# Queries of the differential attention turned by VectorE and DMA, with the scores moved almost a block later

## What is computed

```
k, v = split(rms_norm(x) @ w_kv);  k = rms_norm(k per 128 columns)
q = rms_norm((rms_norm(x) @ w_q) per 128 columns) * 128 ** -0.5
s = q @ k.T + alibi bias, causal;   p = softmax(s)
a = p[component 0] - lambda * p[component 1]
o = a @ v;   o = rms_norm(o per head);   x = x + o @ w_out
```

## Time and profile before

| quantity | value |
|---|---|
| median of 3 runs | 2207.62 us (2207.1 to 2207.95) |
| the profiled execution | 2208.22 us |
| its span, first to last instruction | 2206.4 us |
| TensorE matmul busy | 2194.8 us, 99% |
| VectorE busy | 1235.3 us, 56% |
| ScalarE busy | 1057.9 us, 48% |
| granted TensorE clock, mean | 1.00 |

### The profile page before, as it was taken

How to read it: one execution, slowest core, us unless ns; L and a number is a source line. 1 busy time by engine, 2 the same in 40 slices (tenths; PEclk the granted TensorE clock), 3 DMA queues, 4 the chain that set the end, 5 groups by cost and what they waited for, 6 DMA issues and landing times.

```text
span 2206.4 us, 27194 instructions
## 1 busy us (share of the span) xinstructions
PE 2194.8 (99%) x9766; PEld 1814.4 (82%) x9766; DVE 1235.3 (56%) x1448; ACT 1057.9 (48%) x1428; POOL 38.5 (2%) x66
## 2 busy tenths in 40 slices
PE   8999999999999999999999999999999999999999
PEld 7888778888888888888888888888888888888887
DVE  5666556655555555555566675665555555555443
ACT  5666455444444444444456665554444444444332
POOL 1000000000000000000000000000000000000000
PEclk9999999999999999999999999999999999999999
DMA  7766667776767666666666555677676767666654
GB/s 244 214 193 173 175 211 216 203 216 193 215 200 210 205 203 205 199 206 200 204 198 212 180 157 180 209 221 209 198 214 197 216 192 216 198 214 193 194 193 162
DMA packets 254194, 443.34 MB, mean 201 GB/s; under 512 B 25600, under 2 KB 51168, under 8 KB 254112
## 3 DMA queue, kind: packets, MB, share of 16 engines
q1 hardware_dynamic: 253472, 440.95, 66.4%
q0 software_dynamic: 368, 0.79, 0.2%
q10 hardware_dynamic: 272, 0.52, 0.1%
HBM read 414.37 MB, written 2.10 MB: 189 GB/s over the span
## 4 chain that ended last, share of the span: by engine, by line
PE 97%; DVE 1%; DMA 1%; SPq 0%; ACT 0%; issue 0%; DVEq 0%; ACTq 0%
PE acc L603 32%; PE acc L605 32%; PE acc L604 32%; PE tps L614 0%; PE side L807 0%; DMA x<-in_x 0%; DVE w_lo L1246 0%; DVE g_oT L1280 0%; DMA tok<-g_r 0%; SPq L474 0%; DMA raw<-in_gla_w_in 0%; PE side L652 0%; PE side L705 0%; PE side L687 0%; PE side L805 0%
## 5 line engine op out<-in xcount | busy, mean ns | idle before, releaser
L1246 DVE TENSOR_TENSOR w_lo<-raw,w_hi 128x1024 fp32r<-128x1024 f32 x784 | 954.9, 1223 | 842.0 <-ACT w_hi L879 837.8
L879 ACT ACTIVATE w_hi<-raw 128x1024 fp32r<-128x1024 f32 x784 | 827.6, 1060 | 1009.1 <-PE acc L605 999.8
L603 PE MATMUL acc<-w_hi,xT 128*128 128x512 f32 x2048 | 801.9, 392 | 0.1
L605 PE MATMUL acc<-w_hi,xT 128*128 128x512 f32 x2048 | 797.9, 390 | 0.0
L604 PE MATMUL acc<-w_lo,xT 128*128 128x512 f32 x2048 | 797.8, 390 | 0.0
L603 PEld LDWEIGHTS acc<-w_hi,xT 128*128 128x128 f32 x2048 | 385.0, 188 | 80.6 <-issue 1.2
L605 PEld LDWEIGHTS acc<-w_hi,xT 128*128 128x128 f32 x2048 | 384.9, 188 | 80.5
L604 PEld LDWEIGHTS acc<-w_lo,xT 128*128 128x128 f32 x2048 | 385.1, 188 | 80.0 <-issue 0.7
L605 PE MATMUL acc<-w_hi,hT 128*128 128x512 f32 x704 | 273.9, 389 | 0.0
L604 PE MATMUL acc<-w_lo,hT 128*128 128x512 f32 x704 | 273.9, 389 | 0.0
L603 PE MATMUL acc<-w_hi,hT 128*128 128x512 f32 x704 | 273.9, 389 | 0.0
(11 more groups left out here) (179 smaller groups left out, 1048.8 us busy)
## 6 DMA issues: line engine op xcount, KB each, us to landing
raw<-in_ffn_w_in SPq DMA_DIRECT2D x352, 512.0 KB, 4.1
raw<-in_ffn_w_out SPq DMA_DIRECT2D x176, 512.0 KB, 4.9
raw<-in_gla_w_in SPq DMA_DIRECT2D x96, 512.0 KB, 4.2
raw<-in_w_kv SPq DMA_DIRECT2D x64, 512.0 KB, 4.4
raw<-in_gla_w_out SPq DMA_DIRECT2D x32, 512.0 KB, 5.0
raw<-in_diff_w_q SPq DMA_DIRECT2D x32, 512.0 KB, 4.8
raw<-in_diff_w_out SPq DMA_DIRECT2D x32, 512.0 KB, 5.0
tok<-scratch SPq DMA_DIRECT2D x496, 32.0 KB, 3.2
```

The source lines that it names most:

```text
L603: nc.tensor.matmul(acc[p][tb][:, :], hi, w_hi[:, slot, j, :], start=(kt + j == 0), stop=False)
L605: last = nc.tensor.matmul(acc[p][tb][:, :], lo, w_hi[:, slot, j, :], start=False, stop=(kt + j == n_kt - 1))
L879: nc.scalar.activation(w_hi[:, slot, :, :], raw[:, slot, :, :], ACT.Copy).then_inc(hi_done, 1)
L1246: nc.vector.tensor_tensor(w_lo[:, slot, :, :], raw[:, slot, :, :], w_hi[:, slot, :, :].bitcast(F32), ALU.subtract).then_inc(lo_done, 1)
```

## The change

The queries now take the keys' path: VectorE transposes squares of `tok` into a new buffer `q_squares`, 16 DMAs for each block move them into `d_v`, and ScalarE copies them to `d_q`, at (6,3), (7,3), (8,3) and (9,3). TensorE's 32 transposes of queries are gone. The scores, softmaxes and exponentials of even heads move from (5..8, 6) to (6..8, 5) and (9,6), those of odd heads from (6..8, 1) and (9,0) to (7..10, 1) on TensorE (VectorE and ScalarE: (b,2), before (9,0) for the last). The turning of the weights moves from (6..8, 5) and (9,3) to (7..10, 5). The first value product, `diff_output(0)`, moves from (9,2) to (9,3), and the second from (10,1) to (10,3), their squares to (9,4) and (10,4); `diff_o_out` moves from k = 4 to k = 5. Since the last scores now stand between the value products, `scores(6)` waits for `o_tok` of `diff_output(0)`, and `diff_output(1)` for `s_max` of softmax(7). The squares of the first value product go into `q_squares`, because `scratch` still serves the softmaxes.

```diff
+    for n in range(4):
+        units["diff_q", n] = UNIT0["diff_in"] + UB * (n + 5) + 1
     for n in range(3):
-        units["diff_o", n] = UNIT0["diff_in"] + UB * (9 + n) + 4
+        units["diff_o", n] = UNIT0["diff_in"] + UB * (9 + n) + 5
...
+            if name == "diff_q":
+                return qs_in, k_at[n % 2]
+            if name == "diff_o" and n == 0:
+                return qs_in, squares_at
...
                 if h % 2 == 0:
-                    for half in range(2):
-                        pe.wait_ge(t_free[half], PAIR["diff_q", h // 2] + 1)
+                    pe.wait_ge(k_turned, 4 + h // 2 + 1)
+                if h == 6:
+                    pe.wait_ge(o_tok, H_G + 1)
...
-                if n == 0:
-                    pe.wait_ge(s_max, H_D)
+                if n < 2:
+                    pe.wait_ge(s_max, (6, H_D)[n])
                 else:
                     pe.wait_ge(o_tok, H_G + n)
...
-                    if 6 <= b <= 9 and k == (1 if b < 9 else 0):
-                        scores(2 * (b - 6) + 1)
-                    if b >= 9 and k == (2 if b == 9 else 1):
+                    if 7 <= b <= 10 and k == 1:
+                        scores(2 * (b - 7) + 1)
+                    if b >= 9 and k == (3 if b < 11 else 1):
                         diff_output(b - 9)
...
-                    if 6 <= b <= 9 and k == (5 if b < 9 else 3):
-                        probs_turn(b - 6)
-                    if 5 <= b <= 8 and k == (4 if b < 6 else 3):
-                        pe.wait_ge(evacuated[(b - 1) % 2], evac_count("diff_in", b - 1))
-                        transpose_block(PAIR["diff_q", b - 5], tok)
-                    if 5 <= b <= 8 and k == 6:
-                        scores(2 * (b - 5))
+                    if 7 <= b <= 10 and k == 5:
+                        probs_turn(b - 7)
+                    if 6 <= b <= 9 and k == (5 if b < 9 else 6):
+                        scores(2 * (b - 6))
...
                     if k == 3 and 2 <= b <= 5:
-                        k_out(b - 2)
+                        heads_out("diff_k", b - 2, d_k, "k")
+                    if k == 3 and 6 <= b <= 9:
+                        heads_out("diff_q", b - 6, d_q, "q_scaled")
...
-                if n < 4:
-                    dve.wait_ge(evacuated[n % 2], evac_count("diff_in", n))
-                    if n:
-                        all_moved(dve, "diff_k", n - 1)
-                    turn("diff_k", n, lambda tb: tok[:, tb, :])
+                dve.wait_ge(evacuated[n % 2], evac_count("diff_in", n))
+                name, j = ("diff_k", n) if n < 4 else ("diff_q", n - 4)
+                if j:
+                    all_moved(dve, name, j - 1)
+                turn(name, j, lambda tb: tok[:, tb, :])
...
-                    if 10 <= b and k == 4:
+                    if 10 <= b and k == 5:
                         turned_low("diff_o", b - 10, d_oT, diff_o_gain)
-                    if 9 <= b and k == 4:
+                    if 9 <= b and k == 5:
                         diff_o_out(b - 9)
```

More of the change, by code:

```diff
@@ L81, in transpose_jobs @@
     order += [("ffn0_x", 3, True)]
[L82 to L85, removed]
+    order += [("probs", n, False) for n in range(4)]
     pair, split = {}, {}
@@ L139 @@
 TURN = {job: n for n, job in enumerate(TURN_UNIT)}
-TURN_SPLIT = {job: n for n, job in enumerate(job for job in TURN_UNIT if job[0] not in ("gla_qk", "diff_k"))}
+TURN_SPLIT = {job: n for n, job in enumerate(job for job in TURN_UNIT if job[0] not in ("gla_qk", "diff_k", "diff_q"))}
 XQ_SPOT = [(2, 6), (3, 6), (0, 5), (0, 7)]
@@ L275, in trunk @@
             d_oT = sb("d_oT", [P, 2, KT, S], F32R, s1)
+            q_squares = sb("q_squares", [P, TB * CB], F32, s1)
         acc = [[ctx.enter_context(nc.psum_tensor(f"acc{p}{tb}", [P, CB], F32)) for tb in range(TB)] for p in range(2)]
@@ L378, in trunk @@
         k_at = [landing(d_v[:, n, :, :]) for n in range(2)]
+        qs_in = leaving(q_squares[:, :])
         q_in = leaving(d_q[:, 0:TB * CB // S, :].rearrange("q a n -> q (a n)"))
@@ L470, in move_turned @@
                             sp.wait_ge(k_turned, n - 1)
+                        if name == "diff_q":
+                            sp.wait_ge(k_turned, n + 3)
                     if 0 <= first < MOVES:
@@ L1143, in diff_o_gain, with heads_out @@
                 return GAIN["diff_head_scaled"] + kt % 2
-            def k_out(n):
-                all_moved(act, "diff_k", n)
+            def heads_out(name, n, dst, gain):
+                all_moved(act, name, n)
                 for tb in range(TB):
-                    dst = d_k[:, 4 * n:4 * n + 4, tb * P:(tb + 1) * P].rearrange("q k (s t) -> q k s t", t=SQ)
-                    last = nc.scalar.activation(dst, turned(tb, k_at[n % 2]), ACT.Copy, scale=gains[:, GAIN["k"]:GAIN["k"] + 1])
+                    at = dst[:, 4 * n:4 * n + 4, tb * P:(tb + 1) * P].rearrange("q k (s t) -> q k s t", t=SQ)
+                    last = nc.scalar.activation(at, turned(tb, k_at[n % 2]), ACT.Copy, scale=gains[:, GAIN[gain]:GAIN[gain] + 1])
                 last.then_inc(k_turned, 1)
@@ L1195, in _ @@
                         diff_v_out(b - 9)
-                    if 6 <= b <= 9 and k == (2 if b < 9 else 0):
-                        row_exps(2 * (b - 6) + 1)
-                    if 9 <= b and k == (3 if b == 9 else 2):
+                    if 7 <= b <= 10 and k == 2:
+                        row_exps(2 * (b - 7) + 1)
+                    if 9 <= b and k == (4 if b < 11 else 2):
                         diff_o_squares(b - 9)
[L1200 to L1207, removed]
-                    if 10 <= b and k == 4:
+                    if 7 <= b <= 10 and k == 6:
+                        probs_out(b - 7)
+                    if 10 <= b and k == 5:
                         turned_high("diff_o", b - 10, d_oT, diff_o_gain)
@@ L1212, in _ @@
                             xq_high(n)
-                    if 5 <= b <= 8 and k == 6:
-                        row_exps(2 * (b - 5))
+                    if 6 <= b <= 9 and k == (5 if b < 9 else 6):
+                        row_exps(2 * (b - 6))
                     split_ahead(UNIT0["diff_in"] + b * UB + k)
@@ L1370, in scores_out @@
                 nc.vector.tensor_copy(g_at[:, h, 2, :], side[0][:, 3 * P:4 * P]).then_inc(at_free, 1)
-            def tok_is_free(pair):
-                for half in range(2):
-                    dve.wait_ge(t_done[half], pair + 1)
             def gla_o_out(h):
@@ L1547, in qk_norm @@
                 dve.wait_ge(g_rstd_ready, n + 1)
-                if n >= 5:
-                    tok_is_free(PAIR["diff_q", n - 5])
                 for tb in range(TB):
@@ L1607, in diff_o_out @@
                 if n == 0:
-                    tok_is_free(PAIR["diff_q", 3])
+                    all_moved(dve, "diff_q", 3)
                 dve.wait_ge(o_rstd_ready, H_G + n + 1)
@@ L1630, in _ @@
                         qk_norm(b - 1)
-                    if 6 <= b <= 9 and k == (2 if b < 9 else 0):
-                        softmax(2 * (b - 6) + 1)
-                    if 10 <= b and k == 4:
+                    if 7 <= b <= 10 and k == 2:
+                        softmax(2 * (b - 7) + 1)
+                    if 10 <= b and k == 5:
                         turned_low("diff_o", b - 10, d_oT, diff_o_gain)
-                    if 9 <= b and k == 4:
+                    if 9 <= b and k == 5:
                         diff_o_out(b - 9)
@@ L1639, in _ @@
                             xq_low(n)
-                    if 5 <= b <= 8 and k == 6:
-                        softmax(2 * (b - 5))
+                    if 6 <= b <= 9 and k == (5 if b < 9 else 6):
+                        softmax(2 * (b - 6))
                     split_ahead(UNIT0["diff_in"] + b * UB + k)
```

## The result

The changed kernel takes 2212.2 us, median of 12 runs (2209.78 to 2213.74), against 2207.61 us of before (12 runs): ratio 1.0019, 95% interval 1.0011 to 1.0026. It is a small loss, 4.6 us (2.4 to 5.7 by the interval), clear of no change; the bound of 0.2% that I had set for "slower" lies inside the interval. The forecast was 2211.4.

A forecast was written before the change was run, and what follows sets the result against it. TensorE, busy 99% of the span and holding 97% of the chain, was taken as the bound. Waits of 7.25 us against 3.5 us removed gave +3.75 us, so 2207.62 + 3.8 = 2211.4 us, range 2208.8 to 2213.6.

The forecast's parts named there:

- What is removed: Four turnings of queries, 0.87 us each, leave TensorE: 3.5 us off; nothing else leaves it.
- rival 3: Each TensorE transpose is worth its 272 ns duration, so 32 are 8.7 us: 2206.2 us; chance 0.02.
- The waits of the value products: diff_output(0) at (9,3) and diff_output(1) at (10,3) wait for s_max of the softmax: 2.2 us each, 4.4 us.
- The waits for the weights of the softmax: TensorE's turning of weights waits at (7,5) for 0.95 us and at (8,5) for 1.2 us.
- scores(6): At (9,6) TensorE waits for tok of diff_output(0): 0.7 us.
- Sum: Over the five TensorE waits: 7.25 us of waits against 3.5 us removed, +3.75 us.
- rival 4: TensorE's clock falls in the two 2.2 us waits, 1.8 us for each warming: 2215 us; chance 0.05.
- rival 1: Weight loads come late for ScalarE in block 9, 1 to 2 us in one or two places: 2213.2 us; chance 0.14.

The follow-up runs named there:

- order only: Changed kernel's late order, but queries still turned by TensorE with 32 transposes, no squares or small DMAs for them: 2213.76 us, 1.0029 of before.
- the doubled squares: Changed kernel with VectorE's transposes of squares done twice for the queries of blocks 6 and 7, the extra ones read by nobody: 2215.86 us, 1.0033 of before.
- the waits filled: Changed kernel with nine 128x128 float32 matmuls of the identity, read by nobody, ahead of each of the first two value products: 2210.72 us, 1.0017 of before.

## Why the prediction was right

**What is removed.** Four turnings at 0.87 us, 3.5 us. Measured where no wait is left: 3.68 us in the phase, 0.92 each. The distance between instructions was the right reading, not their 272 ns; rival 3 would have given 8.7 us.

**The waits of the value products.** 2.2 us each forecast, 2.13 + 0.1 measured, and 4.40 us back when both are taken away. The row of block 6 that showed the maxima 2.04 us behind TensorE, at a place where nobody cared, was the whole argument. The reverse check, order only, gave 5.01 us for these two and scores(6), of 5.1.

**The waits for the weights of the softmax.** 0.95 and 1.2 us forecast, 0.99 both measured. The second was oversized: I let ScalarE begin the squares of block 8 1.5 us after its start. They began at 1288.12, the block at 1286.89, 1.2 us after it. That VectorE has no slack is shown by the doubled squares.

**scores(6).** 0.7 us forecast, 0.62 + 0.1 measured.

**Sum.** 7.25 - 3.5 = 3.75 forecast for the profiled execution, 3.43 measured in its phase. The wait at (8,5) was put 0.2 too high and what is removed 0.2 too low; both errors made the sum too slow. The rest of that execution was 0.8 us shorter than in before, ahead of the phase.

**The term that was missing.** The sum had no term for the clock. It stood as rival 4 with 1.8 us for a fall and a chance of 0.05, as if it happened always or never. It happens in some executions: below 1.000 in 10 of 23 of the changed kernel, in 0 of 11 with the waits filled. At 1.6 us for a fall that is 0.7 us on the average. I left it out because the only midstream wait of before was 0.37 us late and no row had one of 2 us. The Trainium skill (TensorE: Matmul & The Clock Gate, part 1) warns of idle gaps between bursts; the traces agree in kind: of the five profiled executions with waits of 2.1 us before the value products, two show a fall behind the first of them.

This term does not close the account of the median, and the median does not ask for it. The mean of the 23 executions is 2212.1 us, of all 70 of before 2207.75. These 4.4 us compare with 3.43 of the phase and 0.7 of the falls, 4.1 together. But the 13 executions at 1.000 have a median of 2211.84, already 4.1 to 4.2 above before, and the ten at 0.999 only 0.9 more. The forecast of 3.8 us and the 3.43 of the phase lie both inside the interval of 2.4 to 5.7; what separates them from 4.6 is not clear of noise. That the forecast came within 0.8 us of the median is partly luck, since the errors of the sum and the missing falls go opposite ways.

**What fell away** is rival 1: ScalarE waited for no weight load in the phase, and landings stayed at 6.2 us or less.

## What to carry to other kernels

Where one engine is busy throughout, a change that takes work off it is worth what the order of the others allows. Look for each new wait in the old trace: here the signal and the place both existed already, and their distance was the wait, even where nobody waited yet. Moving the side work by a unit or two at a few places turned a loss of 4.6 us into a gain of 3.6. Compare such kernels by the length of one phase in the traces, which agreed here with hand sums within 0.3 us where no clock fall stood in it, while single runs scatter by 2 to 4.

## What the runs showed of the hardware

A 2.1 us wait of TensorE in midstream can bring its clock from 2.4 to 1.2 GHz for about 3.4 us, at a cost of 1.6 us, and does so in some executions and not in others. Kernels with two such waits had 17 of 42 executions below 1.000, the one with four 6 of 6, and those whose idle waits in the phase are of 1 us at most or none, before included, 7 of 102. That the place of the wait in time decides whether a fall comes was not tested. The waits of 1 us at (7,5) and (8,5) brought no more falls than before has: 2 of 33 executions of the three kernels that have them and no longer idle wait, against 5 of 58.

Eight float32 transposes of 128x128 in a row take 0.9 us of TensorE's sequence, 32 of them 3.68 us, though each is shown with 272 ns.
